# Memories and parameters stored by feature, weights stored as one contiguous block per piece, in a two-stage transformer kernel on one core

## The reference, cut to what matters

```
h = _rmsnorm(x, g_mix[l])
... = jnp.split(h @ w_in[l], offsets, axis=-1)
y_xa = _memory_cross_attention(xa_q, _rmsnorm(mem, g_mem[l]), w_mem_kv[l], xa_g_q[l], xa_g_k[l])
merged = (gates[:, :, 0] * (y_sb @ w_sb_out[l]) + gates[:, :, 1] * (y_ml @ w_ml_out[l]) + gates[:, :, 2] * (y_xa @ w_xa_out[l]))
x = x + merged @ w_o[l]
x = x + (jax.nn.silu(u_gate) * u_val) @ w_down[l]
```

## Time and profile before

| what | value |
|---|---|
| median of 3 runs | 1054.83 us |
| profiled execution | 1052.53 us, its span 1050.7 us |
| TensorE busy | 1030.6 us, 98% of the span |
| TensorE weight loads | 922.0 us, 88% |
| VectorE busy | 730.9 us, 70% |
| ScalarE busy | 654.1 us, 62% |
| moved by DMA | 167.52 MB in 97,831 packets, mean 159 GB/s |
| granted TensorE clock | 0.997 of full |

### The profile page before, as it was taken

The page is one execution under the profiler, slowest core; times in us unless marked ns, Lnnn a source line. Parts: engine busy times, 40 slices in busy tenths (PEclk is TensorE's granted clock), DMA queues, the critical chain, the costliest instruction groups (busy, mean ns, idle before and its releaser), DMA issues.

```text
span 1050.7 us, 19082 instructions
## 1 busy us (share of the span) xinstructions
PE 1030.6 (98%) x8048; PEld 922.0 (88%) x8048; DVE 730.9 (70%) x1085; ACT 654.1 (62%) x924; POOL 13.3 (1%) x18
## 2 busy tenths in 40 slices
PE   6999999999999999999999999999999999999996
PEld 5798987888989999988999998888799999988875
DVE  4684688885747788765565758977884656599686
ACT  6776576564456656544466678657755667776583
POOL 1000000000000000000000000100000000001000
PEclk9999999999999999999999999999999999999999
DMA  8663434666547655566544533422565455344231
GB/s 307 225 202 120 142 124 137 200 200 201 173 149 228 195 179 167 193 223 187 173 160 130 165 125 120 141 83 102 180 199 168 130 161 161 101 143 142 79 116 47
DMA packets 97831, 167.52 MB, mean 159 GB/s; under 512 B 7048, under 2 KB 32530, under 8 KB 97490
## 3 DMA queue, kind: packets, MB, share of 16 engines
q1 hardware_dynamic: 95776, 159.24, 47.3%
q0 software_dynamic: 1472, 5.51, 1.5%
q10 hardware_dynamic: 498, 1.55, 0.4%
HBM read 165.23 MB, written 1.05 MB: 158 GB/s over the span
## 4 chain that ended last, share of the span: by engine, by line
PE 95%; DVE 3%; DMA 1%; ACT 1%; issue 1%; SPq 0%; DVEq 0%
PE proj L598 13%; PE proj L589 13%; PE proj L600 13%; PE proj L599 13%; PE proj L591 13%; PE proj L590 13%; PE mix L935 1%; PE mix L979 1%; PE mix L936 1%; PE mix L634 1%; PE mix L659 1%; PE mix L642 1%; PE mix L968 1%; DVE wlo L1538 1%; DMA raw<-in_w_mem_kv 1%; PE mix L875 1%
## 5 line engine op out<-in xcount | busy, mean ns | idle before, releaser
L1538 DVE TENSOR_TENSOR wlo<-raw,whi 128x1024 fp32r<-128x1024 f32 (+3 forms) x303 | 355.4, 1202 | 139.9 <-ACT whi L1065 138.0
L1065 ACT ACTIVATE whi<-raw 128x1024 fp32r<-128x1024 f32 (+3 forms) x303 | 306.2, 1040 | 148.1 <-PE proj L600 66.5
L589 PE MATMUL proj<-act_hi,whi 128*128 128x256 f32 x1064 | 303.5, 285 | 0.6 <-ACT arena L1082 0.4
L591 PE MATMUL proj<-act_hi,wlo 128*128 128x256 f32 x1064 | 300.9, 283 | 0.0
L590 PE MATMUL proj<-act_lo,whi 128*128 128x256 f32 x1064 | 300.9, 283 | 0.0
L589 PEld LDWEIGHTS proj<-act_hi,whi 128*128 128x128 f32 x1064 | 203.1, 191 | 3.3 <-ACT arena L1082 1.2
L590 PEld LDWEIGHTS proj<-act_lo,whi 128*128 128x128 f32 x1064 | 203.2, 191 | 0.9
L591 PEld LDWEIGHTS proj<-act_hi,wlo 128*128 128x128 f32 x1064 | 203.2, 191 | 0.2
L598 PE MATMUL proj<-whi,y_hi 128*128 128x512 f32 (+1 forms) x340 | 135.1, 397 | 3.8 <-DVE wlo L1538 3.5
L599 PE MATMUL proj<-wlo,y_hi 128*128 128x512 f32 (+1 forms) x340 | 132.4, 389 | 0.0
L600 PE MATMUL proj<-whi,y_lo 128*128 128x512 f32 (+1 forms) x340 | 132.3, 389 | 0.0
(11 more groups left out here) (360 smaller groups left out, 1239.7 us busy)
## 6 DMA issues: line engine op xcount, KB each, us to landing
raw<-in_w_in SPq DMA_DIRECT2D x144, 512.0 KB, 4.4
raw<-in_w_up SPq DMA_DIRECT2D x88, 256.0 KB, 4.2
raw<-in_w_out SPq DMA_DIRECT2D x32, 512.0 KB, 4.3
raw<-in_w_down SPq DMA_DIRECT2D x22, 512.0 KB, 5.4
raw<-in_w_mem_kv SPq DMA_DIRECT2D x8, 512.0 KB, 9.1
raw<-in_w_mem_k SPq DMA_DIRECT2D x8, 512.0 KB, 4.0
raw<-in_w_o SPq DMA_DIRECT2D x8, 512.0 KB, 3.7
raw<-in_w_mem_v SPq DMA_DIRECT2D x8, 512.0 KB, 3.9
```

Of the source, the lines that this page charges most:

```text
L589: mm(o, wh[:, i, wc], hi[:, k0 + i, :], start=begin and j % 2 == 0, stop=False, skip_group_check=True)
L591: last = mm(o, wl[:, i, wc], hi[:, k0 + i, :], start=False, stop=end, skip_group_check=True)
L1065: fn(whi[c % SPLIT][:, 0:w], raw[c % SLOTS][:, 0:w], ACT.Copy).then_inc(s.w_hi, 1)
L1538: tt(wlo[c % SPLIT][:, 0:w], raw[c % SLOTS][:, 0:w], f32(whi[c % SPLIT][:, 0:w]), ALU.subtract).then_inc(s.w_lo, 1)
```

## The change

The host hands over other arrays (`laid_out`); on the chip the following changes.

- `mem` and `mem_2` come by feature, [128 partitions, 8 feature blocks, 256 tokens]. The 16 transposes of `mem` and the 2 x 16 of `mem_2` are gone. ACT rounds straight from SBUF (`mem_upper`, 8 instructions for `mem`, one of 128x2048 for each `mem_2`), DVE makes the lower part in the same way (`mem_lower`).
- The sums of squares of `mem` now run over partitions: ACT squares all of it (128x2048), DVE adds over the 8 feature blocks, and TensorE adds over the partitions by two small matmuls with a column of ones, between `xak` and `xav`.
- All parameters come as one array `params` by one DMA of 1096 bytes for each partition on ACT's queue; their transposes and copies are gone. ACT's queue now carries the identity, too.
- Every piece of weights is one contiguous block of 512 KB (4 KB for each partition), one DMA each, those of `w_up` too.
- SyncE's order at the start is: first half of `mem`, pieces 0 and 1, second half of `mem`, pieces 2, 3, 4, then `x`. POOL's table and the rest wait until 16 pieces are split. ACT's other constants are fetched after `leave_mem("xav")`.
- `x` is transposed in the middle of `xav` instead of ahead of it, and the square roots' logarithm waits for the two small matmuls.
- The rounding of the table, the logarithms and the sines, and DVE's chain for them, go from ahead of `xaq` to after the shares of the first attention, ahead of `leave("sbv")`.

```diff
@@ SyncE
-            sp.dma_start(const[:, 0:P], a["const"][:, 0:P]).then_inc(s.ident_in, 16)
-            for b in range(NB):
-                sp.dma_start(MEM[:, b, :], a["mem"][0, b * P:(b + 1) * P]).then_inc(s.mem_in, 16)
             for c, loads in enumerate(pieces):
-                if c == SLOTS:
+                if c in (0, 2):
+                    half = slice(c * KT // 4, c * KT // 4 + KT // 2)
+                    sp.dma_start(MEM[:, half, :], a["mem"][:, half, :]).then_inc(s.mem_rest if c else s.mem_in, 16)
+                if c == SLOTS + 1:
                     sp.dma_start(X[:, :, :], a["x"][0].rearrange("(b p) d -> p b d", p=P)).then_inc(s.x_in, 16)
                 if c >= SLOTS:
                     sp.wait_ge(s.w_lo, c - SLOTS + 1)
                 k, n = dims[c]
-                view = raw[c % SLOTS][:, 0:k * n].rearrange("p (k c) -> p k c", c=n)
-                for src, _, cols, shift in loads:
-                    sp.dma_start(view[:, :, shift:shift + cols], src).then_inc(w_loaded[c % SLOTS], 16)
+                src = a["weights"][begins[c]:begins[c + 1]].rearrange("(p c) -> p c", c=k * n)
+                sp.dma_start(raw[c % SLOTS][:, 0:k * n], src).then_inc(w_loaded[c % SLOTS], 16)
@@ GpSimd
-            pool.wait_ge(s.x_in, 16)
+            pool.wait_ge(s.w_lo, 4 * SLOTS)
             pool.dma_start(TREE_IN[:, :], a["tree"]).then_inc(s.tree_in, 16)
@@ TensorE
+            project("xak", None, MEM_hi, MEM_lo, ready=lambda k: pe.wait_ge(s.mem_lo, k))
+            pe.wait_ge(s.mem_sum, 1)
+            for b in range(NB):
+                last = mm(mix[:, 3, 4 * b:4 * b + 4], MEM_SUM[:, b * P:(b + 1) * P], ONE4, start=True, stop=True)
+            last.then_inc(s.mem_ss, 1)
+            project("xav", None, MEM_hi, MEM_lo, part=(0, 2))
+            pe.wait_ge(s.norm_x, 1)
             pe.wait_ge(s.ident_in, 16)
...
+            turn(KT, lambda k, b: XN[:, b, k * P:(k + 1) * P])
+            project("xav", None, MEM_hi, MEM_lo, part=(2, 4))
...
-            pe.wait_ge(s.mem2_in, 16)
-            turn(KT, lambda k, b: MEM2_AT[None][:, b, k * P:(k + 1) * P])
@@ ScalarE
+            act.dma_start(par[:, :], a["params"]).then_inc(s.params, 16)
+            act.dma_start(const[:, 0:P], a["const"][:, 0:P]).then_inc(s.ident_in, 16)
...
+            act.wait_ge(s.params, 16)
+            act.wait_ge(s.mem_in, 16)
+            mem_upper(range(KT // 2))
             split_until(2)
+            act.wait_ge(s.mem_rest, 16)
+            mem_upper(range(KT // 2, KT))
+            split_until(SLOTS)
+            fn(MEM_SQ, MEM, ACT.Square).then_inc(s.mem_sq, 1)
+            split_until(SLOTS + 1)
...
+            split_until(SLOTS + 2)
+            fn(FIRST_R[:, 2:4], FIRST_SS, ACT.Ln, bias=epsb[:, 0:1], scale=1.0 / DM)
+            act.wait_ge(s.mem_ss, 1)
...
+            attend_exp(0, XP, XA_D ** -0.5)
+            split_until(ahead_of("sbv", None, 1))
             act.wait_ge(s.tree_in, 16)
             fn(tree[:, :, :, :].rearrange("p b l t -> p (b l t)"), TREE_IN, ACT.Copy).then_inc(s.tree_ok, 1)
...
-            turned("mem2", None, KT, MEM_hi, lambda k: 1.0)
+            act.wait_ge(s.mem2_in, 16)
+            fn(MEM_hi, MEM2_AT[None], ACT.Copy).then_inc(s.mem2_hi, 1)
@@ VectorE
-            turned("mem2", None, KT, MEM_hi, MEM_lo, None).then_inc(s.mem2_ok, 1)
+            dve.wait_ge(s.mem2_hi, 1)
+            tt(MEM_lo, MEM2_AT[None], f32(MEM_hi), ALU.subtract).then_inc(s.mem2_ok, 1)
```

More of the change, by code:

```diff
@@ L1 @@
 import contextlib
+import itertools
 import math
@@ L85, with by_column, laid_out @@
 PI = 3.1415925
+def by_column(*rows):
+    return np.concatenate([v.reshape(-1, P).T for v in rows], 1)
+PARAM_NAMES = {"block1": ("g_mix", "g_mem", "g_ffn", "ml_conv_w", "ml_conv_b"), "ffn": ("ff_conv_w", "ff_conv_b"),
+               "heads": ("xa_g_q", "xa_g_k", "hgrn_out_norm_2", "mla_q_norm_2", "mla_kv_norm_2"), "logits": ("hgrn_lb_logits_2",)}
+PARAMS = {"block1": 0, "ffn": 8 * KT, "heads": 8 * KT + 8 * FT, "logits": 8 * KT + 8 * FT + 10,
+          "bias": 10 * KT + 8 * FT + 10, "end": 10 * KT + 8 * FT + 18}
+def laid_out(inputs):
+    named = {name: np.asarray(inputs[name]) for name in _INS}
+    arrays = {name: np.ascontiguousarray(named[name]) for name in _WHOLE}
+    bias = np.concatenate([named["ml_b_i"][0], named["ml_b_f"][0]])
+    columns = [by_column(*(named[name] for name in names)) for names in PARAM_NAMES.values()]
+    arrays["params"] = np.ascontiguousarray(np.concatenate([*columns, np.broadcast_to(bias, (P, 2 * ML_H))], 1))
+    for name in ("mem", "mem_2"):
+        arrays[name] = np.ascontiguousarray(named[name][0].T.reshape(KT, P, SEQ).transpose(1, 0, 2))
+    arrays["positions"] = np.ascontiguousarray(named["positions_2"][0].reshape(NB, P).T)
+    arrays["weights"] = packed(named)
+    arrays["const"], arrays["tree"] = CONST, TREE
+    return arrays
 def piece(w, row, k, col, n):
-    return [(w[row:row + k * P, col:col + n].rearrange("(k p) c -> p k c", p=P), k, n, 0)]
+    return [((*w, row, col), k, n, 0)]
 def piece_dims(loads):
@@ L331, in stack_kernel, with packed @@
                 pieces.append(shape[to][n])
+    return place, number, shape, pieces
+def packed(named):
+    flat = []
+    for loads in schedule()[3]:
+        k, cols = piece_dims(loads)
+        to = np.empty((P, k, cols), np.float32)
+        for (name, L, row, col), _, n, shift in loads:
+            to[:, :, shift:shift + n] = named[name][L][row:row + k * P, col:col + n].reshape(k, P, n).transpose(1, 0, 2)
+        flat.append(to.reshape(-1))
+    return np.concatenate(flat)
+def stack_kernel(nc, a, out):
+    place, number, shape, pieces = schedule()
     dims = [piece_dims(loads) for loads in pieces]
     loaded, per_slot = [], [0] * SLOTS
+    begins = [0, *itertools.accumulate(P * k * n for k, n in dims)]
     for c, loads in enumerate(pieces):
-        per_slot[c % SLOTS] += 16 * len(loads)
+        per_slot[c % SLOTS] += 16
         loaded.append(per_slot[c % SLOTS])
@@ L1145, in _, with mem_upper @@
             nc.scalar.preload_act_table(ACT.Copy)
-            act.wait_ge(*stage(1, None))
-            turned("mem", None, KT // 2, MEM_hi, lambda k: cols1[:, 1, k:k + 1])
-            split_until(1)
-            turned("mem", None, KT // 2, MEM_hi, lambda k: cols1[:, 1, k:k + 1], KT // 2)
-            split_until(2)
-            FIRST_SS, FIRST_R = stat[:, 232:236], stat[:, 236:240]
+            def mem_upper(tiles):
+                for k in tiles:
+                    fn(MEM_hi[:, k, :], MEM[:, k, :], ACT.Copy, scale=cols1[:, 1, k:k + 1]).then_inc(s.mem_hi, 1)
@@ L1165, in leave_mem @@
+            act.wait_ge(s.mem_ss, 1)
+            link(fn(FIRST_R[:, 0:2], mix[:, 3, 0:8].rearrange("p (b c) -> p b c", c=4)[:, :, 0], ACT.Ln, bias=epsb[:, 0:1], scale=1.0 / DM))
+            fn(FIRST_R, FIRST_R, ACT.Exp, scale=-0.5).then_inc(s.norm_r, 1)
+            split_until(pieces_until("xak", None))
             def leave_mem(name, dst):
```

240 lines of the change are left out of this document (99 added, 141 removed).

## The result

The kernel after takes 1055.24 us (median of 20 runs, 1052.29 to 1058.4), the kernel before 1053.55 us in the same series (20 runs, 1051.39 to 1055.42). The ratio is 1.0017, 95% interval 1.001 to 1.0024: 0.17% slower, less than the 0.3% named above, where 0.8% faster was forecast. The profiled execution took 1054.21 us, its span 1052.4.

The account below looks back on a forecast made before the run. TensorE, busy 98% of the span, bounds the kernel. 3.4 + 1.1 + 2.9 + 1.4 - 0.3 - 0.3 - 0.5 = 7.7 us off 1052.5 gives 1044.8, as a median 1047.1; 1046 was taken, range 1041 to 1051.

Parts of the forecast that it names:

- What bounds the kernel now: Opening step, whole kernel: TensorE is busy 98% of the span; only its lost instructions or idle stretches win time.
- crumbs: TensorE's list of waits: what remained beside 3.5 us for DVE's lower parts and 0.8 us ahead of the mLSTM part.
- Transposes of the second memory: Two sites, near 224.69 and 588.56 us: 16 transposes fewer at each win 3.4 us (0 to 3.5).
- the transposes covered something: Rival, behind both second-memory sites: TensorE meets waits for late DVE and ACT, 3.4 us come back, 1049.5 us; chance 0.10.
- Transposes of the parameters: TensorE between the last matmul of `xav` and the first of `xaq`: 1.1 us go.
- First projection: Start of the kernel: first matmul at 9.3 instead of 12.21 us, 2.9 us won (0.9 to 3.8).
- The hole in `xav`: TensorE's standstill at 29.16 to 30.81 us, for late piece 6: 1.4 us go (0 to 1.4).
- Two small matmuls: Added on TensorE for the sums of squares of `mem`: cost 0.3 us (0 to 1).
- Block of ACT and DVE ahead of `leave("sbv")`: After the first attention's exponentials: 5.4 us of ACT work makes the copy out of `sbv` 0.5 us late (0 to 2).
- Contiguous pieces: All weight loads: 0 us, as long as a piece lands within 8.5 us.
- Constants and table collide: Rival at 40 to 54 us: they delay piece 16, TensorE stands 4.8 us; 1051 us, 1049 at half; chance 0.18.
- if its busy time falls by less than 4: Sign, whole kernel: the prediction is wrong if TensorE's busy time falls by less than 4 us.

Follow-up runs that it names:

- the spread version: Changed kernel plus 121 TensorE instructions: 160 idle waits ahead of `xak`, two behind each of the next 41 groups of three matmuls; 1046.63 us, ratio 0.9932.
- with 135 more: Kernel before with 135 more TensorE instructions, idle waits: 85 ahead of its first instruction, 50 after the transposes of `mem`; 1067.29 us, ratio 1.0145.
- the two runs on it: Changed kernel with strided pieces (2 KB runs) again: 1055.36 us, ratio 1.0033; kernel before with contiguous pieces only: 1052.07 us, ratio 0.9996.

## Why the prediction was wrong, step by step

**The step that failed** is in "What bounds the kernel now": "a microsecond is won only where TensorE loses an instruction or an idle stretch". Each instruction taken away was booked as its own time and nothing more. No term, bound or rival had a cost of *where TensorE's other instructions come to lie*. That cost is +6.6 us, by the alignment from 590 us (-4.95) to the end (+1.7): holes of 7.8 us in all in the kernel after, against 0.68 and 0.51 in the kernel before. The kernel before's waits for issue, 0.8 us, stood in its list of waits and went under "crumbs". The rivals looked for late neighbours (loads, ACT, DVE); the one that came is the supply of TensorE's own program, which the page shows as 0.4% of the DMA engines' time.

That the rest was about right shows in the spread version, which has all of the change and the borders of the kernel before: 1046.63 us, 7.1 below the 1053.75 of the kernel before beside it, where the sum said 7.7. That the two are so near is partly luck: the spans of the two traces differ by 5.5 us only (1050.7 and 1045.2), of which 0.5 come from a hole of the kernel before that is gone, while a low stretch that the sum didn't have took 1.5 away. The terms, by the traces:

- *Transposes of the second memory*, 3.4 us: measured 1.77 and 1.22 by alignment, 3.0. Behind the second site TensorE now waits 0.3 us for ACT (L1369), which it didn't before: a little of the rival "the transposes covered something" came true.
- *Transposes of the parameters*, 1.1 us: the step to `xaq` is now 36.76 - 36.53 = 0.23 us. Right.
- *First projection*, 9.3 us: 10.14, 0.8 late, of 2.9 us 2.1 won. Half of `mem` and the parameters were to be there at 4.8; ACT began at 6.18, released by the parameters. With them first it began at 5.80, for `mem`: the loads at the start share the DMA engines, and I had let them come one after another.

The two rows of ACT, first in the kernel after:

```profile
6.18 1.70 ACT L1169 ACTIVATE y_hi<-arena,par 128x256 fp32r<-128x256 f32 x4 [3.23 <-DMA par<-in_params]
```

```profile
5.80 1.70 ACT L1176 ACTIVATE y_hi<-arena,par 128x256 fp32r<-128x256 f32 x4 [3.33 <-DMA arena<-in_mem]
```

- *The hole in `xav`*, 1.4 us: gone. Right.
- *Two small matmuls*, 0.3 us: 23.97 - 23.61 = 0.36. Right.
```profile
10.00:12.00 2.00, 1.86 (x4) 1.49 (x5) 2.00 (x5) 1.95 (x5) 0.00 (x0) 1.00 0.99 375
12.00:14.00 2.00, 2.00 (x6) 1.60 (x5) 2.00 (x5) 2.00 (x3) 0.00 (x0) 1.00 0.99 389
14.00:16.00 2.00, 2.00 (x7) 1.55 (x7) 1.61 (x2) 2.00 (x2) 0.00 (x0) 1.00 0.99 391
...
182.00:184.00 2.00, 2.00 (x7) 1.49 (x6) 2.00 (x7) 1.99 (x2) 0.00 (x0) 0.65 0.91 287
184.00:186.00 2.00, 2.00 (x6) 1.52 (x6) 1.34 (x5) 1.97 (x3) 0.00 (x0) 0.50 0.86 320
```

  The Trainium skill (TensorE: Matmul & The Clock Gate, "Part 1: The HAM clock gate") has the engine begin throttled until it is active. The traces agree: 0.43 us a matmul from the first one on, and full speed from the first projection where matmuls ran before it (there the first rise is recorded at 6.12 us).
- The last two rows are a cost that I didn't have: a low stretch at 183 us, 1.5 us. Nine of the twelve kernels with the change show it, and one of the three in the order of before (with 135 more). TensorE had no wait ahead of it, but its last work there is 2 us of eight small matmuls of 4x256 (180.26 to 182.23 us in the kernel after), and in all ten the clock falls at their end or up to 1.4 us later. The other five have the same matmuls and no fall. Why stays open.
- *Block of ACT and DVE ahead of `leave("sbv")`*, 0.5 us: no wait of TensorE stands there. 0.
- *Contiguous pieces*, 0 us: right, by the two runs on it. *Constants and table collide*: no wait at `sbk`'s transposes. *The transposes covered something*: no wait behind the first site, 0.3 us behind the second.

By -3.5 us at `xaq` and -3.0 for the second memory, the working part came to 6.5 us of 7.7. The busy time fell by 5.6 us, so the sign "if its busy time falls by less than 4" stayed away, and the time still rose: idle time for issue wasn't among the signs that I named.

**What stays open.** Shown are the place of the holes, that moving the count modulo 256 moves them, that one instruction can open or close one, and that each ends 1.2 to 1.6 us behind a packet. Why a packet starts when it does, at 150 used instructions in one block and at 200 in another, isn't known, nor what made some packets take 1.4 us instead of 0.9. Nor is it known why the clock falls behind some holes and at 183 us in some kernels.

## What to carry to other kernels

After a change, read TensorE's waits for "issue" first: a few microseconds there, inside dense bursts of small matmuls that the edit didn't touch, were the instruction blocks here. Then time the change with the old number of instructions (idle waits in an idle stretch) before judging it; here that turned +0.17% into -0.7%. Where a long idle start can't be avoided, matmuls on a constant tile until the first data are ready save the slow first stretch, 2.3 us here, and can carry the padding too.

## What the hardware showed unexpectedly

- TensorE's program comes in blocks of 256 instructions (16,384 bytes) during the execution. A burst of 320 instructions in 1.3 us can outrun them: up to 2.2 to 2.8 us of standstill, or as little as none, by where the blocks end.
- Taking out 121 instructions cost 6.6 us; putting back 121 that do nothing won 8.6 us in the median (1055.24 to 1046.63) and 7.2 between the two traces (spans of 1052.4 and 1045.2).
- TensorE passed the fixed place of a block never earlier than 1.2 us after the end of its packet, in 15 traces; a packet took 0.9 to 1.5 us next to the holes.
- One instruction decided over 3.0 us by the traces and 4.1 in the median, about half of it through the clock, which fell to its lower level behind the 2 us hole.
